# Two weight blocks of a product taken together while its row tiles are still being made

## The reference

```
for i in range(DEPTH_2):                       # 4 layers: gla, mla, conv, gla
    h = mixer_i(x)                             # ends with a product with its w_out
    x = layer_norm(ALPHA * x + h, ln_g[i, 0], ln_b[i, 0])
    x = layer_norm(ALPHA * x + sq_relu_mlp(x, mlp_w1[i], mlp_w2[i]), ln_g[i, 1], ln_b[i, 1])
    x = x + sigmoid(x @ ple_w_gate[i]) * (p[i] @ ple_w_proj[i])
```

## Time and profile before

| | |
|---|---|
| median of 3 executions | 3547.14 us (3544.69 to 3548.5) |
| the profiled execution's own time | 3550.65 us |
| its span in the trace | 3549.0 us |
| granted TensorE clock, mean over the span | 0.938 of full |
| TensorE matmuls busy | 3209.3 us, 90% of the span |
| DVE busy | 1750.9 us, 49% |
| ACT busy | 1384.8 us, 39% |

### The profile page before, as it was taken

The page is one execution under the profiler, slowest core; times in us unless marked ns, Lnnn a source line. Parts: engine busy times, 40 slices in busy tenths (PEclk is TensorE's granted clock), DMA queues, the critical chain, the costliest instruction groups (busy, mean ns, idle before and its releaser), DMA issues. The chain is left out here.

```text
span 3549.0 us, 51646 instructions
## 1 busy us (share of the span) xinstructions
PE 3209.3 (90%) x20788; PEld 2785.9 (78%) x20788; DVE 1750.9 (49%) x2632; ACT 1384.8 (39%) x2232; POOL 195.6 (6%) x287
## 2 busy tenths in 40 slices
PE   6999988889999899988799788996899989988898
PEld 4777856557778588867599677996699989976898
DVE  3332353553323533254655437666575686653765
ACT  3222231532222322233454425544454555441544
POOL 1111014001110000003000000000000000000000
PEclk8999999999999999999999978998899999996999
DMA  7555333035554222334145423643165545441452
GB/s 242 166 165 167 107 113 92 13 107 166 166 168 140 81 97 95 126 100 134 48 152 180 130 84 107 190 160 109 48 197 183 159 146 187 158 149 48 142 186 100
DMA packets 403815, 471.08 MB, mean 133 GB/s; under 512 B 9660, under 2 KB 381964, under 8 KB 403626
## 3 DMA queue, kind: packets, MB, share of 16 engines
q1 hardware_dynamic: 380176, 389.05, 34.4%
q0 software_dynamic: 22592, 79.07, 7.1%
q10 hardware_dynamic: 858, 0.29, 0.0%
HBM read 467.20 MB, written 1.20 MB: 132 GB/s over the span
## 5 line engine op out<-in xcount | busy, mean ns | idle before, releaser
L424 DVE TENSOR_TENSOR w_lo<-w_raw,w_hi 128x1024 fp32r<-128x1024 f32 x734 | 896.9, 1227 | 1316.2 <-ACT w_hi L421 1315.0
L432 PE MATMUL bank<-a_hi,w_hi 128*128 128x256 f32 (+1 forms) x3864 | 1247.0, 323 | 147.1 <-DVE a_lo L1572 51.3
L433 PE MATMUL bank<-a_lo,w_hi 128*128 128x256 f32 (+1 forms) x3864 | 1232.8, 319 | 0.0
L434 PE MATMUL bank<-a_hi,w_lo 128*128 128x256 f32 (+1 forms) x3864 | 1231.0, 319 | 0.0
L421 ACT ACTIVATE w_hi<-w_raw 128x1024 fp32r<-128x1024 f32 x734 | 772.1, 1058 | 1032.6 <-PE bank L434 1013.2
L432 PEld LDWEIGHTS bank<-a_hi,w_hi 128*128 128x128 f32 x3864 | 745.9, 193 | 226.6 <-issue 151.3
L433 PEld LDWEIGHTS bank<-a_lo,w_hi 128*128 128x128 f32 x3864 | 748.1, 194 | 48.8 <-issue 0.5
L434 PEld LDWEIGHTS bank<-a_hi,w_lo 128*128 128x128 f32 x3864 | 744.6, 193 | 50.4
L432 PE MATMUL bank<-h_hi,w_hi 128*128 128x256 f32 (+1 forms) x1728 | 546.5, 316 | 0.0
L433 PE MATMUL bank<-h_lo,w_hi 128*128 128x256 f32 (+1 forms) x1728 | 539.8, 312 | 0.0
L434 PE MATMUL bank<-h_hi,w_lo 128*128 128x256 f32 (+1 forms) x1728 | 539.3, 312 | 0.0
(11 more groups left out here) (286 smaller groups left out, 2596.8 us busy)
## 6 DMA issues: line engine op xcount, KB each, us to landing
w_raw<-in_mlp_w SPq DMA_DIRECT2D x128, 1024.0 KB, 5.5
w_raw<-in_w_ffn_gate_up SPq DMA_DIRECT2D x88, 1024.0 KB, 5.2
m_raw<-in_w_mod POOLq DMA_DIRECT2D x128, 512.0 KB, 4.8
w_raw<-in_w_ffn_down SPq DMA_DIRECT2D x32, 1024.0 KB, 6.0
w_raw<-in_gla_w_in SPq DMA_DIRECT2D x24, 1024.0 KB, 5.3
w_raw<-in_w_in SPq DMA_DIRECT2D x16, 1024.0 KB, 5.9
w_raw<-in_ple_w_gate SPq DMA_DIRECT2D x16, 1024.0 KB, 5.1
w_raw<-in_w_ffn_down SPq DMA_DIRECT2D x16, 768.0 KB, 5.6
```

The source lines that it names most:

```text
L424: e.tensor_tensor(lo, raw, hi.bitcast(F32), ALU.subtract).then_inc(S.lo_ready.sem, 1)
L432: e.matmul(dst, hi, rhs_hi, start=start, stop=False)
L433: e.matmul(dst, hi, rhs_lo, start=False, stop=False)
L434: return e.matmul(dst, lo, rhs_hi, start=False, stop=stop)
```

## The change

First, a new function `two_slots` does the slots p = 0 and p = 1 of a product in one interleaved run: step k of the second slot stands three steps behind step k of the first. `gemm` uses it where a table `ready` is given, the matrix is one slot deep, and no modulation product is mixed in (`mod_per == 0`). Second, the cut that stood at the end of `product_norm` moves up into its loop, to the end of step k = 3.

```
+            def two_slots(n, kt, rhs, dsts, ready, evicted):
+                behind = 3
+                for j in range(kt + behind):
+                    for s, k in ((0, j), (1, j - behind)):
+                        if not 0 <= k < kt:
+                            continue
+                        if s == 0 and k in ready:
+                            e.wait_ge(ready[k][0].sem, ready[k][1])
+                        if s == 1 and k == 0:
+                            e.wait_ge(S.act_evicted.sem, evicted[0])
+                            e.wait_ge(S.dve_evicted.sem, evicted[1])
+                        r_hi, r_lo = rhs(k)
+                        for m in range(2):
+                            if k == 0:
+                                e.wait_ge(S.lo_ready.sem, 2 * (n + s) + m + 1)
+                            mm = three(dsts[2 * s + m], cut_slot(w_hi, n + s)[:, k, m * P:m * P + P],
+                                       cut_slot(w_lo, n + s)[:, k, m * P:m * P + P], r_hi, r_lo, k == 0, k == kt - 1)
+                            if k == kt - 1:
+                                mm.then_inc(S.slot_used.sem, 1)
...
-                            if pe:
+                            together = ready is not None and each == 1 and mod_per == 0 and i is None and p < 2
+                            if pe and together and p == 0:
+                                two_slots(n, kt, rhs, b_ap(bank[0:4]), ready, last)
+                            if pe and not together:
...
                         if k < 4:
                             centre_tile(k + 4)
                             centred[k + 4] = S.dve.n
+                        if k == 3:
+                            ahead(last_slot, None, 0, (1,))
...
                 at.a_ready = done
-                ahead(last_slot, None, 0, (1,))
```

## The result

| | before | changed |
|---|---|---|
| median, 13 executions each | 3545.18 us (3530.46 to 3556.78) | 3565.41 us (3558.15 to 3580.98) |
| the profiled execution, and its span | 3550.65, 3549.0 us | 3575.34, 3573.6 us |
| granted clock, mean over the span | 0.938 | 0.932 |

The ratio is 1.0068 with a 95% interval of 1.0049 to 1.0087: slower by 20.2 us between the medians, 24.6 us between the two profiled spans. The forecast was 3572.0 us, in a range of 3556 to 3580.

A forecast was written before the change was run, and what follows sets the result against it. TensorE, with matmuls for 90% of the span, was taken as the bound. Eight norms at 3.3 us (+26.4) less 1.6 for layer 1's mixer gave +24.8 on the 3547.14 us median: 3571.9 us, range 3556 to 3580.

The forecast's parts named there:

- The pause: At each of 8 norms TensorE stands still 2.55 us for tile 1, whose `a_lo` is queued behind `w_lo`.
- The chain up to the start of `a_lo[1]`: At the first norm: ACT's `xt[3]`, `w_hi`, then DVE's `w_lo`; `a_lo[1]` starts at about 2188.45 to 2188.52, formerly 2185.61.
- The last link: At the norm, TensorE picks up tile 1 0.73 us behind the start of its `a_lo`, as with tile 0.
- waits of 2.2 to 2.9 us and 20 in all: Sign in the trace: a second PE wait on `a_lo` at each of 8 norms, some 20 us together.
- The restart: Behind each norm's new wait the first matmul is followed after 0.35 us, not 0.21: 0.14 more.
- The clock: Behind each norm the half-clock stretch counts from the second restart; tile 0's six half-clock matmuls come on top: 0.6 us.
- The rival in which the clock rises at the old moment: Behind norms, part of the pause falls into half-clock time and costs less: +11.4 us, 3558.5 us; chance 0.13.
- The sum: Whole kernel: 8 norms x 3.3 = +26.4, mixer of layer 1 -1.6, the other seven places nothing: +24.8 us.
- The mixer: Mixer of layer 1: the second block fills TensorE's idle time between tiles, gaining 1.6 us, bounded by 0.8 and 2.7.
- The cover of slot n + 2: Slot n + 2's cut still fits, 0.2 us to spare, priced at nothing; rival: it fails, 5 us, chance 0.06.
- the last rival: The earlier cut removes TensorE's waits for `w_lo`, at most 13.5 us in 6 waits: faster, 3532 us; chance 0.04.
- What is taken away at the norm's end is no help: At the norm's end `w_lo` was already done at 2192.04, before TensorE reached the second slot at 2193.55.

The follow-up runs named there:

- Experiments 2: The kernel before with only the cut moved into the norm's loop at k = 3, no interleave: 3568.23 us, ratio 1.0085.
- experiment 4: The changed kernel with `w_hi` written early, right behind the Sqrt, and `w_lo` still in front of `a_lo[1]`: 3555.82 us, ratio 1.0044.
- (1): The changed kernel with the cut put back at the norm's end, so the interleave alone: 3556.08 us, ratio 1.0053 against the kernel before.
- experiment 8: The kernel before with 27 added matmuls of ones, result unused, behind each norm's last sum: 3537.61 us, ratio 1.0002.
- experiment 12: The kernel of experiment 8 timed a second time, on another chip: 3535.62 us against 3534.01 for the kernel before, ratio 1.0004.
- experiment 5: The kernel before with 50 added matmuls of ones, result unused, behind each norm's last sum: 3554.48 us, ratio 1.0044.
- experiment 9: The changed kernel with 27 added matmuls of ones behind each norm's last sum: 3558.88 us, ratio 1.0059 against the kernel before.

## Why the prediction was right

**The pause.** It is where and what the forecast said: `w_lo` in front of `a_lo[1]`, held up by ACT. From the first matmul of tile 0 to that of tile 1 it is 3.73 us against 1.42, so 2.31 a norm; the forecast had 2.55. The chain up to the start of `a_lo[1]` was right: 3.20 us behind TensorE's start (2187.21 less 2184.01), forecast 3.23 to 3.30. The last link was mis-sized: from there to TensorE it is 0.53 us, and I had taken 0.73 from tile 0. DVE's idle time in it is 1.58 us (forecast 1.6). I had looked for waits of 2.2 to 2.9 us and 20 in all; they are 2.12 and 17. Experiments 2 and 4 show the cause: the moved cut alone brings the pause, and with `w_hi` early most of it goes.

**The restart.** 16 restarts instead of 8, with 5.82 us to the next matmul instead of 2.81: 0.36 us each, 0.16 us a norm over the 0.21 of a slow matmul (forecast 0.14).

**The clock.** In the eight stretches of 96 distances between starts, 216 are at half clock (192 plain ones, 16 restarts, 8 pauses) where 165 were before (157 and 8): 51 more, 6.4 a norm, where I had said six. What is left of the sum is 24.47 less 8 x 2.31 less 8 x 0.16 = 4.7 us, 0.58 a norm (forecast 0.6). It is a remainder, but it fits: 51 x 0.1 us are 5.1, and the changed kernel has fewer matmuls at the slower of two speeds at full clock (last section). The rival in which the clock rises at the old moment, which would have given 3558.5, is excluded by the windows above (6.6 to 9.8 us against 2.9 to 6.2). The Trainium skill, "TensorE: Matmul & The Clock Gate", Part 1, has it that the warm-up is an amount of time and not a number of matmuls. No run here can tell the two apart, since slow matmuls stand 0.21 us apart in both kernels. What a pause does to the warm-up is read from the trace alone: 37.5 us at half clock from the second restarts, 35.5 from the first ones before.

**The sum.** Per norm 2.31 + 0.16 + 0.58 = 3.05 instead of 3.3, so 24.4 instead of 26.4. The mixer gave 1.95 instead of 1.6. Its bounds in the forecast were misread, though: of the eight waits in the earlier trace rows five are weight loads, and the matmuls' own are 7.32, 0.60 and 0.21 us. The 2.7 us weren't idle time between tiles, and the 1.95 are more than the 0.81 that was. A matmul counts as busy to its modelled end, so a part of the time lost between tiles shows only in the distance of the starts. That 1.6 came so near is luck. Forecast +24.8, measured +24.6 between the profiled spans. Part of that agreement is luck, since two executions of one kernel differ by more than the errors of the terms.

**The cover of slot n + 2.** It held behind the norm: half 0 is evicted at 2198.17 and its `w_lo` is done at 2200.76 (2199.53 + 1.23), and TensorE needs it at 2201.15 (2184.01 plus the 17.14 us of this norm's 96 matmuls), 0.39 us later. All waits for `w_lo` together are 15.0 us in 8, from 13.5 in 6. Nearly all of both are weight loads; the matmuls' own waits in them are 1.4 us, from 0.5, so the last rival's ceiling of 13.5 us was much too high. One of these waits is new, 0.40 us at 2422.48, at the start of slot n + 2 of a product behind `cut_x`: there the cover failed, and that I had put at nothing.

```profile
2198.17 0.39 ACT L1613 ACTIVATE tmp_g<-bank 128x256 f32<-128x256 f32 x1 [6.74 <-PE bank L434]
...
2199.53 1.23 DVE L424 TENSOR_TENSOR w_lo<-w_raw,w_hi 128x1024 fp32r<-128x1024 f32 x1 [0.52 <-ACT w_hi L421]
```

**What the earlier cut is good for.** "What is taken away at the norm's end is no help" holds for the kernel before, where no norm had a wait for `w_lo`. What I didn't see is that the interleave itself makes one, 12.6 us without the moved cut (1). Seen from there the changed kernel pays 24.4 us to save 12.6 that only its other half makes necessary.

**The median.** Predicted 3572.0, measured 3565.41. The median of before had itself been 3547.14 in three executions and is 3545.18 in thirteen; the difference of the medians, 20.2 us, is below the 24.6 of the profiled pair, within what the interval of 1.0049 to 1.0087 (17 to 31 us) leaves.

**What stays open.** The 27 matmuls take 11 us from the norms in both profiled executions (94.6 and 95.2 us, from 106.2), and in the timed ones the granted clock is higher each time: 0.946 to 0.950 in the twelve of experiment 8, against 0.938 to 0.942 in the 23 of before beside them. Yet the time is the same twice (1.0002, 1.0004). Something gives back 11 us outside the norms. The last section has a candidate that is large enough, but nothing here ties it to the added matmuls.

## What to carry to other kernels

Each engine goes through its list in order, so "this can be prepared earlier" means "this stands in front of something": look for what is queued behind it on each engine that it occupies, and ask when the input of the second engine's part is ready. Here the two halves of one cut wanted different places, and moved as one piece they stopped TensorE for 2.3 us at each of eight norms. A second block of work between two tiles pays only where TensorE is idle between tiles, and at half clock it isn't: the trace of before showed one such place in sixteen, and it gained 2 us. And when a block of weights comes free later, the transfers behind it move too: at one other place a wait for a table became 3 us shorter with it, likely for that reason, and 1 us of this was left further on.

## What the runs showed of the hardware

**Two speeds at full clock.** Within one execution the same 256-column matmuls start either 0.1133 or 0.1178 us apart, 4% of each other, through whole stretches in which PEclk is 1.00. Two windows of the same length in the kernel before, behind its first and its fifth norm, (PE's count is the first in brackets):

```profile
2205.00:2235.00 30.00, 30.00 (x267) 30.00 (x266) 21.74 (x34) 18.36 (x36) 0.00 (x0) 1.00 0.66 199
...
2913.00:2943.00 30.00, 30.00 (x258) 30.00 (x256) 21.32 (x34) 17.39 (x32) 0.00 (x0) 1.00 0.62 188
```

The changed kernel, the first of these windows:

```profile
2205.00:2235.00 30.00, 30.00 (x257) 30.00 (x256) 22.59 (x35) 17.76 (x33) 0.00 (x0) 1.00 0.71 211
```

267 matmuls in 30 us, or 257. Which of the two it is changes from norm to norm and from execution to execution of the same kernel: of some 8900 of the second stack's 256-column matmuls at full clock (blocks of 48, sorted by their mean distance) about 41% go at the slower speed in experiment 8 (span 3527.4 us) and about 76% in experiment 12 (span 3550.0 us), which is the same kernel. The difference, some 3200 matmuls at 0.0045 us, is an estimated 14 of the 22.6 us between these spans. That explains a good part of why one kernel spreads over 20 us and more, and why two profiled spans alone don't measure a change of 10 us. What sets the speed I don't know; the granted clock doesn't show it. Nor do the added matmuls seem to: the share is 27 to 52% in the six profiled kernels without them and 19 to 76% in the eight with them.

**An f32 matmul of 128 columns leaves two records**, 0.111 us apart at full clock (the 50 of experiment 5 are 100 records, the 27 of experiment 8 are 54), where each float32r matmul of 256 columns is one record, 0.113 us from the next.

**The clock falls in a short pause.** With TensorE busy up to tile 0 and at full clock, 2.79 to 2.81 us of idle time were enough for the matmuls behind it to go at half clock (experiment 9, at all eight norms); 0.38 us were not (experiment 8). At four of the eight the granted clock falls only 0.1 to 0.4 us behind the restart. At the wait for `g_carry` full clock outlasted 2.0 to 2.7 us of idle time in all eight kernels that have it so short, 2.73 us in experiment 4, and with 4.5 us and more it was lost. The length of a pause alone therefore settles little between 2.0 and 2.8 us.
